# Half-token tiles around the norms of a transformer kernel, with the residual factor folded into X

## What is computed

```python
def deepnorm_residual(x, y, g, b):
    return layer_norm(DEEPNORM_ALPHA * x + y, g, b)

def ffn_sublayer(x, shift, scale, gate, w_gu, w_down, g, b):
    y = swiglu(modulate(x, shift, scale), w_gu, w_down)
    return deepnorm_residual(x, MACARON_WEIGHT * gate * y, g, b)

for layer in range(2):
    x = ffn_sublayer(x, ...);  ctx = ffn_sublayer(ctx, ...)
    h_lat, h_ctx = modulate(x, ...), modulate(ctx, ...)
    o_lat, o_ctx = even_mixer(...) if layer == 0 else odd_mixer(...)
    x = deepnorm_residual(x, gate * o_lat, ...)
    x = ffn_sublayer(x, ...)
    # layer 0 alone: the same two steps for ctx
```

## Time and profile before

| | |
|---|---|
| median of 3 runs | 2883.29 us (2880.13 to 2885.84) |
| profiled execution | 2885.58 us, its span 2883.8 us |
| mean granted TensorE clock | 0.949 |
| instructions | 43361 |
| weight halves split (L1884) | 1024 from the ring, 16 first ones |
| bytes moved | 352.85 MB, 122 GB/s in the mean |

### The profile page before, as it was taken

How to read it: one execution, slowest core, us unless ns; L and a number is a source line. 1 busy time by engine, 2 the same in 40 slices (tenths; PEclk the granted TensorE clock), 3 DMA queues, 4 the chain that set the end, 5 groups by cost and what they waited for, 6 DMA issues and landing times.

```text
span 2883.8 us, 43361 instructions
## 1 busy us (share of the span) xinstructions
PE 2680.6 (93%) x16824; PEld 2313.4 (80%) x16824; DVE 1731.7 (60%) x2978; ACT 1260.8 (44%) x2390; POOL 671.8 (23%) x608
## 2 busy tenths in 40 slices
PE   8999997988788999999999988989979999899998
PEld 5887886867776888887888867789978988898888
DVE  5775666778766765556554555565544656346666
ACT  3332326531255333334333345655545575454673
POOL 1111111012134111112111121021134424555224
PEclk9999998998788999998999988999979999899999
DMA  6553441210002543433443422245524434334334
GB/s 252 184 175 115 153 154 44 81 59 2 2 16 74 179 168 127 144 128 117 161 153 124 168 81 74 81 139 184 183 88 135 145 109 133 131 132 139 117 104 138
DMA packets 115868, 352.85 MB, mean 122 GB/s; under 512 B 12752, under 2 KB 14928, under 8 KB 115280
## 3 DMA queue, kind: packets, MB, share of 16 engines
q1 hardware_dynamic: 115664, 350.08, 36.1%
HBM read 348.98 MB, written 1.05 MB: 121 GB/s over the span
## 4 chain that ended last, share of the span: by engine, by line
PE 72%; DVE 12%; ACT 7%; issue 5%; POOL 3%; DMA 1%; SPq 0%; DVEq 0%; ACTq 0%; POOLq 0%
PE ps L1570 20%; PE ps L1572 19%; PE ps L1571 19%; ACT spl L1884 2%; PE ps L1620 2%; DVE spl L2120 1%; DVE big L2330 1%; PE ps L1636 1%; DVE work L2307 1%; PE ps L1838 1%; PE ps L1630 1%; DVE work L2225 1%; ACT big L2061 1%; POOL bigr L2584 1%; PE ps L1581 1%
## 5 line engine op out<-in xcount | busy, mean ns | idle before, releaser
L1570 PE MATMUL ps<-bigr,spl 128*128 128x256 f32 (+1 forms) x3880 | 1344.2, 346 | 69.9 <-issue 21.2
L1571 PE MATMUL ps<-bigr,spl 128*128 128x256 f32 (+1 forms) x3880 | 1313.4, 339 | 0.0
L1572 PE MATMUL ps<-bigr,spl 128*128 128x256 f32 (+1 forms) x3880 | 1312.9, 338 | 0.0
L2120 DVE TENSOR_TENSOR spl<-ring,spl 128x512 fp32r<-128x512 f32 x838 | 678.0, 819 | 652.8 <-ACT spl L1884 650.2
L1884 ACT ACTIVATE spl<-ring 128x512 fp32r<-128x512 f32 x1024 | 623.6, 625 | 763.8 <-PE ps L1572 606.2
L1570 PEld LDWEIGHTS ps<-bigr,spl 128*128 128x128 f32 x3880 | 750.4, 193 | 182.3 <-issue 44.7
L1571 PEld LDWEIGHTS ps<-bigr,spl 128*128 128x128 f32 x3880 | 752.4, 194 | 75.0 <-issue 2.2
L1572 PEld LDWEIGHTS ps<-bigr,spl 128*128 128x128 f32 x3880 | 750.9, 194 | 76.4
L2584 POOL TENSOR_TENSOR bigr<-work,bigr 128x512 fp32r<-128x512 f32 (+1 forms) x200 | 210.8, 1060 | 1026.5 <-ACT bigr L1888 1026.4
L2579 POOL TENSOR_TENSOR spl<-ring,spl 128x512 fp32r<-128x512 f32 x186 | 254.3, 1369 | 361.2 <-ACT spl L1884 360.9
L1888 ACT ACTIVATE bigr<-work 128x512 fp32r<-128x512 f32 (+2 forms) x232 | 120.5, 522 | 317.9 <-DVE work L2202 169.2
(11 more groups left out here) (291 smaller groups left out, 2506.6 us busy)
## 6 DMA issues: line engine op xcount, KB each, us to landing
ring<-w_stream SPq DMA_DIRECT2D x512, 512.0 KB, 3.4
big<-w_stream SPq DMA_DIRECT2D x256, 256.0 KB, 3.0
big<-w_stream SPq DMA_DIRECT2D x16, 512.0 KB, 11.0
X<-x_t SPq DMA_DIRECT2D x2, 1024.0 KB, 13.7
cst<-consts SPq DMA_DIRECT2D x1, 1601.5 KB, 7.3
X<-mem_t SPq DMA_DIRECT2D x1, 1024.0 KB, 5.7
out_t<-X SPq DMA_DIRECT2D x8, 128.0 KB, 2.1
prm<-params SPq DMA_DIRECT2D x1, 252.5 KB, 2.7
```

The costliest lines, as they stand in the source:

```text
L1570: pe.matmul(out, hi, x[0], start=k == 0, stop=False)
L1571: pe.matmul(out, hi, x[1], start=False, stop=False)
L1572: finish(pe.matmul(out, lo, x[0], start=False, stop=k == nk - 1), tile, key if k == nk - 1 else None)
L2120: dve.tensor_tensor(lo_half(h), raw_half(h), hi_half(h), SUB).then_inc(*sig("lo", h, by="lo_dve"))
```

## The change

It does the following, and `NCH`, the number of weight chunks, goes from 656 to 701.

- **`out_halves`**: the last two down tiles of `ffn(0..2)` and the last six output tiles of the even mixer are computed first for tokens 0 to 255, all of them, and then again for tokens 256 to 511, with the weights taken a second time. In the second pass `pace` advances the norm of the first half at k-steps 9 (column sums and root), 17 (spreads) and 20, 23, ... 41 (k = 0 to 7 of the norm).
- **`in_halves`**: the next stage opens with six tiles (three gate/up pairs, or ab, qkv 0, glu value and gate 0, z 0 and 1) for the first half of the tokens, 48 k-steps, paced in the same way with the norm of the second half; then the same six for the second half, with the weights taken again. The odd mixer does so with two key tiles, the values and two query tiles.
- **`Norm.steps(e)`**: subtract, multiply, modulate and `dual` over 256 tokens; the modulation is on DVE for even k and on ACT for odd k.
- **`residual`**: one DVE instruction per half, bank times gate plus X, read from the bank; ALPHA is put into X beforehand, by `alpha_cols` and `ln_update`, for the first stage by `first_scale` on ACT.
- **`sqrt_table`**: a root of one column on ACT before the down or output tiles.
- **`conv_silu`**: the silu of a short convolution is yielded one tile later. z tiles 0 and 1 and both glu tiles 0 move to the front of the even mixer.
- `pos["auto"]`: the late side work is spread over 28 pumps instead of 36, with 30 calls in the six down tiles that are left.
- **`load_memory`** waits for the modulations that read X, no more for `ln_update`.

```diff
+            def half_tile(key, w, bank, free, src, tick=None):
+                for k, (hi, lo, need) in enumerate(src):
+                    tile = yield from take(w(k))
+                    yield "linear", key, bank, free, k, len(src), tile, (hi, lo), need, L
+                    if tick:
+                        yield from tick()
+            def pace(gen):
+                count = [0]
+                at = {9, 17} | {20 + 3 * k for k in range(KD)}
+                def tick():
+                    count[0] += 1
+                    if count[0] in at:
+                        yield from advance(gen)
+                return tick
+            def in_halves(keys, ws, norm):
+                gen = norm.steps(1)
+                tick = pace(gen)
+                all_ = [banks.get() for _ in keys]
+                for (bank, free, bi), w in zip(all_, ws):
+                    yield from half_tile(None, w, bank[:, 0:L], free, norm.src(0), tick)
+                yield from rest(gen)
+                for (bank, free, bi), key, w in zip(all_, keys, ws):
+                    yield from half_tile(key, w, bank[:, L:T], free, norm.src(1))
+                return [(bank, bi) for bank, _, bi in all_]
+            def out_halves(key, ks, w, srcs, gate, sums, xs, norm):
+                gen = norm.steps(0)
+                sums.split()
+                for e in range(2):
+                    a = L * e
+                    tick = pace(gen) if e else None
+                    for k in ks:
+                        bank, free, bi = banks.get()
+                        kk = key + (k,) if e else key + (k, 0)
+                        yield from half_tile(kk, w(k), bank[:, 0:L], free, [(hi[:, a:a + L], lo[:, a:a + L], need) for hi, lo, need in srcs], tick)
+                        x, u = Xt[k][:, a:a + L], new()
+                        yield "residual", u, [(x, bank[:, 0:L], gate[0][:, k, e:e + 1])], [kk, gate[1]], xs[k]
+                        banks.give(bi, ("res_x", u))
+                        yield from sums.add_half(e, x, [("res_x", u)], k == ks[-1])
+                yield from rest(gen)
...
+                def steps(self, e):
+                    a = L * e
+                    G, Bc, key = self.nxt
+                    mean, r = yield from self.sums.finish_half(e, D, "eps5")
...
+                    for k in range(KD):
+                        yield CUT
+                        if k == 0:
+                            yield "ln_sub", u, 0, xh[0], mean[0], need
+                        if k < KD - 1:
+                            yield "ln_sub", u, k + 1, xh[k + 1], mean[0], need
+                        yield "ln_mul", u, k, xh[k], r[0], r[1]
+                        m, mfree, mi = sqs.get()
+                        eng = "dve" if k % 2 == 0 else "act"
+                        yield "half_mod", u, k, m[:, 0:L], xh[k], G[:, k, e:e + 1], Bc[:, k, e:e + 1], [key] + mfree, eng
+                        t = yield from dual(m[:, 0:L], XM[k][0][:, a:a + L], XM[k][1][:, a:a + L], [("ln_m", u, k)])
...
-                    pos["auto"] = 0, KD * len(late) + 2, 4 * KD + 4
+                    pos["auto"] = 0, KD * len(late) + 2, 28
-                for k in range(KD):
-                    b, bi = yield from linear(("down", f, k), tile_of("ffn_w_down", (l, j), 128 * k), [(H[m][0], H[m][1], [hs[m]]) for m in range(KF)], n)
+                srch = [(H[m][0], H[m][1], [hs[m]]) for m in range(KF)]
+                for k in range(KD if n == L else KD - 2):
+                    b, bi = yield from linear(("down", f, k), tile_of("ffn_w_down", (l, j), 128 * k), srch, n)
                     yield from residual(("down", f, k), b, bi, k, n, gate, sums, xs[k])
                 pos["auto"] = None
                 yield from drain()
...
+                norm = Norm(sums, ln, nxt, T if f < 2 else L)
+                yield from out_halves(("down", f), (KD - 2, KD - 1), lambda k: tile_of("ffn_w_down", (l, j), 128 * k), srch, gate, sums, xs, norm)
+                return norm.xs, norm
...
-                ins.then_inc(*sig("res_t", u))
...
-                dve.scalar_tensor_tensor(x, x, ALPHA, t[:, 0:n], MUL, ADD).then_inc(*sig("res_x", u))
+                for x, b, gate in parts:
+                    ins = dve.scalar_tensor_tensor(x, b, gate, x, MUL, ADD)
+                ins.then_inc(*sig("res_x", u))
```

More of the change, by code:

```diff
@@ L24 @@
 HC = CH // 2
-NCH = 656
+NCH = 701
 NEG = -1.0e30
@@ L426, in linear, with side_by_side @@
                 return bank, bi
-            def pair(key0, key1, w0, w1, src, n, between=None):
-                both = [banks.get() for _ in range(2)]
+            def side_by_side(keys, ws, src, n, between=None):
+                all_ = [banks.get() for _ in keys]
+                ns = n if isinstance(n, tuple) else (n,) * len(keys)
                 for k in range(len(src)):
@@ L440, in by_token, with rest @@
+            def rest(gen):
+                for s in gen:
+                    if s is not CUT:
+                        yield s
             def by_token(key, name, idx, c0, w, xs, src, out, need, between=None):
@@ L461, in spread, with columns @@
                 return b, ("spread", u), bi
-            def columns(n, squares, plain=()):
+            def columns(n, squares):
                 b, free, bi = banks.get()
@@ L783, in even_mixer @@
                 yield "pads", CP.bufs, f0
-                src = [(XM[k][0], XM[k][1], ms[k]) for k in range(KD)]
-                (bab, iab), first = yield from pair(
-                    ("ab",), ("qkv_mm", 0), lambda k: [("even_w_in", (0,), 128 * k, 128, 2048 + 4 * r, 4, 32 * r) for r in range(4)],
-                    tile_of("even_w_in", (0,), 0), src, T)
                 yield "gates_in", bab, f0
@@ L1134, in odd_mixer @@
             def odd_mixer(xs, ms):
-                yield from flush()
+                gen = ms.steps(1)
+                tick = pace(gen)
+                tiles_K = [banks.get() for _ in range(2)]
+                for h, (bank, free, bi) in enumerate(tiles_K):
+                    yield from half_tile(None, tile_of("attn_w_in", (0,), 128 * (8 + h)), bank[:, 0:L], free, ms.src(0), tick)
+                tiles_V = yield from odd_values(0, ms.src(0), tick)
+                bank, free, bi = banks.get()
+                first_q = [(bank[:, 0:L], None), (bank[:, L:T], bi)]
+                for h in range(2):
+                    yield from half_tile(("attn_in", h), tile_of("attn_w_in", (0,), 128 * h), first_q[h][0], free, ms.src(0), tick)
+                yield from rest(gen)
+                yield "load_memory", sum(ms.read, [])
                 f0 = [("down", 2, KD - 1), pos["colsum"]]
@@ L1446, in order, with first_scale @@
                     ms.append([t])
-            xs = [[("x", k // 4)] for k in range(KD)]
+            xs = [[("x_scaled", k)] for k in range(KD)]
+            def first_scale():
+                for k in range(KD):
+                    yield "first_scale", k
+            later.append(first_scale)
             pos["unsplit"] = False
```

314 lines of the change are left out of this document (205 added, 109 removed).

## The result

The changed kernel takes 2972.0 us (median of 4 runs, 2969.16 to 2978.74), beside 2883.98 for the kernel before in the same comparison: ratio 1.031, 95% interval 1.029 to 1.0331. It is slower, as forecast, but by 88 us and not by 33, and lies above the range. Its profiled execution took 2973.01 us, span 2971.2.

A forecast was written before the change was run, and what follows sets the result against it. PE, busy 93% of the span, was taken as the bound. Terms -73.1 + 13.6 + 83 + 5 + 1.7 + 5 + 0 - 3 = +32 on the profiled 2885.6 gave 2918, forecast as median 2916 us, range 2846 to 2938.

The forecast's parts named there:

- the drains: Late side work in `ffn(0)` and `ffn(2)`: four steps left before the halved tiles, PE waits for the sum; +5 (0 to 8).
- the clock falls too: Rival: granted clock drops to 1.2 GHz in paced passes, 5 us for each boundary, 2936 us; chance 0.10.
- The ring: Paced stretches: splits and norm steps wait on each other across DVE and ACT, rounds about 3.2 us; +83 in all.
- The rejected rival: Splits find room in paced passes, DVE and ACT limited by their own work: 16 us of stalls, 2849 us; chance 0.26.
- The pitch of a k-step: Weights taken twice: 340 k-steps whose two 256-column matmuls outlast one of 512 columns by 13.3 ns; +13.6 us PE time.
- The openings: Three `glu` at once, then eight updates, on ACT against 8.2 us of splits ahead; +1.7 once (0 to 4).
- Memory sums: Memory sums now come behind the values, with squares and sums on POOL, and PE waits for them; +5 (0 to 6).
- Even mixer's projections: Silu no longer waits 2.40 us for the convolution, but six results reach ACT at once; 0 (-6 to +4).
- Tables and residual: Root tables earlier and no ACT step in the residual, shortening two norms over 256 tokens; -3 (-5 to 0).
- -73.1: PE time lost at the four norms over 512 tokens, all of which a perfect cover would return: 73.1 us.

The follow-up runs named there:

- e1: Changed kernel with side work paced by its true step count, several steps allowed per call, so nothing is left for the drains: 2945.64 us.
- e10: e6 with the early side work of `ffn(0)` at its true 73 steps, spread over all 68 calls: 2860.85 us, ratio 0.9916.
- e2: Changed kernel with the second part of each weight split yielded one half of weights later than its `hi`, everywhere: 2915.19 us.
- e4: Kernel before the change, with the second part of each weight split yielded one half of weights later: 2929.44 us, ratio 1.0155.
- e3: Kernel before, plus the change's residual, `alpha_cols`, `first_scale`, `sqrt_table` and `conv_silu`, without halved tiles: 2886.37 us, ratio 1.0008.
- e5: Changed kernel with the second part of each split one half of weights later only in the paced stretches: 2905.35 us, ratio 1.007.
- e6: Changed kernel with both the late splits of e5 and the side-work pacing of e1: 2872.97 us, ratio 0.9957.
- e12: Kernel before, with the other half of the second block's splits given to POOL and nothing else changed: 2887.6 us, ratio 1.0007.
- e9: Kernel before, with only the true step numbers for its side work: 2874.74 us, ratio 0.9966.
- e7: e6 with `ffn(0)`'s early side work at its true step count over 60 calls and the eight scalings spread over later tiles: 2870.43 us.

## Why the prediction was right in its sign and wrong in its size

**The step that failed: the drains**, the line "30 calls for 34 steps, so four stay", priced at +5. The mechanism was there, and three counts in it were wrong. The late groups of `ffn(0)` and `ffn(2)` have 37 steps, since a group has nine cuts and not eight: seven stay, not four. `ffn(1)` was taken to have no drain, but its early groups have 64 steps for 60 calls, and it drains before its down tiles. And two multiply steps were priced for each late drain, 3.2 us for two conditions and 1.6 for one, where five stand: ten instructions in `ffn(0)`, 9.29 us, and five in `ffn(2)`, 5.79 us. PE waits 10.18, 4.50 and 6.68 us, 21.4 in place of +5. With what the clock adds behind them the three places cost 30.4 us by e1's stretches, and e1 as a whole is 26.4 us faster. The trace of before couldn't show this, but counting the `CUT`s of the generator would have.

**The second step that failed: no term for the clock.** The forecast left it out, and "the clock falls too" stood as a rival with a chance of 0.10. Counted from the timeline, matmuls of 256 columns that start 0.18 us or more apart with no idle time between them cost 9.2, 6.4, 4.5 and 7.9 us at the four boundaries over their 0.120; 4.1 of these 28 us follow a drain. So some 24 us, 6 a boundary where the rival had 5, are the lower clock behind the ring's stalls. The two rivals that were priced apart, ring and clock, came together.

**The ring: right in kind, and its stalls a little smaller than forecast.** Forecast 20 to 22 a boundary, measured 24.6, 28.1, 21.9 and, at the odd mixer (1736.12 to 1819.40, counted in the same way), 25.1: 99.7 us for 83; but this is elapsed time and holds the 28 us of lower clock. Without them 72 us stand for 83, of which the view of waits records 61 as PE idle. The rounds were priced at 3.1 and 3.3 us and measured 2.92 to 3.57. The rejected rival, DVE and ACT working through with their own work alone, is what e10 shows at last (4.3, 8.1, 2.8 us): the work was never too much for the two engines, only its order. That is near its bound of 2 us a pass, 4 a boundary, but for the even mixer's 8.1. The prediction had named order as what counts against it, and that was right for the change as it stands. The Trainium skill (TensorE: Matmul & The Clock Gate, Architectural detail) has the queues of ACT and DVE strictly first in, first out; the 1.00 and 1.64 us of DVE idle in the rounds agree, and e2 and e4 show both sides of it: a split that stands later in the queue no longer blocks the norm, and is itself blocked by it.

**The pitch of a k-step** held: nine matmuls of 256 columns apart stand the starts 1349.72 and 1350.80 in the changed kernel, 0.120 us each, so 13.6 us stay as priced. No run took them out alone.

**The openings**, priced once at +1.7, cost PE 4.3 us of waits in `ffn(1)` and 4.6 in `ffn(2)`, where three glu come at once and then eight updates. In `ffn(2)`:

```profile
1416.31 0.50 PE L1764 MATMUL ps<-bigr,spl 128*128 128x512 f32 x1 [1.25 <-ACT work L2116]
...
1431.95 0.50 PE L1764 MATMUL ps<-bigr,spl 128*128 128x512 f32 x1 [1.74 <-DVE spl L2315]
...
1450.45 0.50 PE L1764 MATMUL ps<-bigr,spl 128*128 128x512 f32 x1 [0.90 <-DVE spl L2315]
```

The releaser L2116 on ACT is the glu's silu. The first of the two splits had its `hi` behind the eight updates on ACT (5.76 us from 1424.89), the second behind a tile that ACT made at 1447.85. The step should have been counted per boundary.

**Memory sums, +5.** The sum was not waited for (0.55 us). In its place PE waits for the norm of the heads, since the key and query tiles are now done ahead and no projection lies between to hide it:

```profile
1839.20 1.19 PE L2037 MATMUL ps<-big,cst 128*128 128x256 f32 x2 [5.34 <-DVE big L2665]
...
1863.47 0.58 PE L1764 MATMUL ps<-bigr,spl 128*128 128x256 f32 x1 [4.85 <-DVE big L2665]
```

In the kernel before the first of these was 1.56 us and the second was not there, so these two rows are +8.6. But other waits in the same region became shorter: behind the boundary, up to the second block, PE idles 38.7 us in the kernel before (from 1724.15) and 43.0 in the changed one (from 1820.0). So in the balance it is +4.3, near the priced sum by another way. This is read from the two traces; no run separates it, and e10 has both waits still.

**Even mixer's projections, 0 (-6 to +4).** In the changed kernel the stretch is 24.0 us longer; its ring (24.6 - 16.9), pitch (3.7) and drain (13.5 in e1, less 2.6 of slow k-steps that the 24.6 holds already) make 22.3, so the term is near 0, as priced. e3 shows -5.5 without the halves, so the halves seem to take 5 us or more back, though such a difference of two profiles is weak. Six results at once, the effect named against the gain, would fit; it stayed untested.

**Tables and residual, -3:** with the silu's -5.5 inside it, e3 as a whole gives +2 (0 to +5). The ACT step taken out of the residual bought nothing that can be measured.

**The clock, in rows.** The page's mean granted clock is 0.945 against 0.949, and hides this: the old boundaries ran at 0.69 to 0.82, and those losses are gone. In one paced stretch it fell right behind the stalls, 0.92 and then 0.53, which is the lower level, 1.2 GHz, for the 7 us after it:

```profile
1347.00:1371.00 24.00, 15.52 (x114) 0.92 0.25 89
1371.00:1378.00 7.00, 7.00 (x35) 0.53 0.47 150
```

35 matmuls at 0.21 and not 0.12 us are 3 us there. They are inside the 21.9 us of that boundary, as the others are inside theirs. e5 and e6 win them back together with the stalls; no run separates the two.

**The sum again**, with measured terms: -73.1 + 13.6 + 99.7 for the ring with its clock (24.6 + 28.1 + 21.9 + 25.1) + 26.3 for the drains (30.4, less the 4.1 that the 99.7 holds) + 8.9 for the openings + 4.3 behind the odd mixer's boundary = +80. Of 87.4 us between the spans, some 8 stay without a term. 5.7 us lie in the attention of the even mixer, 246.7 us against 241.0, where the granted clock is 0.82 against 0.84. e12, whose instructions up to there are those of the kernel before, took 245.5 us there at 0.80, so a difference of this size comes about between two executions of the same instructions and needs no part of the change. Why the clock differs there is open. 3 lie in the second block, where the parity of the splits alone moves one stretch by 10 us. What is left elsewhere is 1 to 2 us at a place, of either sign.

## What to carry to other kernels

When work is cut into finer pieces and interleaved by hand, walk the queues of the two engines that hand work to each other: if a piece goes DVE, ACT, DVE and a split goes ACT, DVE in the same order, each round costs the sum of both chains, however idle the engines look. Put the second half of such a pair later in its queue, but only in the stretch where the pieces alternate, since elsewhere its lead is what covers a long step ahead of it. When you price stalls, look at the granted clock behind them too: here it made a quarter of what a boundary lost. And where side work is spread over calls by a count, get the count from the generator, and look what a `drain` will find left when a loop is made shorter.

## What the runs showed that was not expected

- A queue position is worth more than the work in it: moving the second part of the split by one half of weights gave 67 us in the paced stretches of the changed kernel (e5) and cost 46 us on the kernel before (e4).
- The old kernel had some 10 us to give without any of this: its side work was counted one step short per group (e9).
- A DVE split of 512 columns takes 0.69 us alone and up to 1.6 beside POOL; which of the two engines takes the odd splits moves the mean in one stretch from 803 to 1167 ns and the stretch by 10 us (e12), and the kernel by 2. The Trainium skill (SBUF — State Buffer, Who interferes with whom) says that a DVE instruction with two inputs in SBUF and a POOL instruction that reads SBUF hold a shared port one at a time; the two means above, 0.69 us for splits that overlap no POOL instruction and 852 to 1253 ns for those that do, agree with that.
- Faster side work may delay the weights, which isn't shown: in e7 ACT waited 60.5 us for chunks between 100 and 320 us, in e10, with 68 calls for 60 and the eight scalings put back, 53.5 us, and the kernel was 10 us faster. The two edits weren't separated.
